# One or two accumulators in memory for the expert blocks of a mixture-of-experts layer

## What is computed

```
def one_block(args):
    tok_b, gate_b, e = args
    xb = xpad[tok_b]
    hb = jax.nn.silu(xb @ w_gate[e]) * (xb @ w_up[e])
    return (hb @ w_down[e]) * gate_b[:, None]

out = lax.map(one_block, ...)
routed = jax.ops.segment_sum(out.reshape(P, D), tok, num_segments=T + 1)[:T]
...
x = x + g2[:, None, :] * (routed + shared).reshape(B, L, D)
...
y = modulate(rms_norm(x, g_final), shf, scf)
```

## Time and profile before

| | us |
|---|---|
| median of 3 runs | 3123.6 (3121.36 to 3126.76) |
| the profiled execution's own time | 3120.24 |
| its span, first to last instruction | 3118.4 |
| PE busy in the span | 2632.8 (84%) |
| DVE busy | 1776.0 (57%) |
| POOL busy | 1143.8 (37%) |
| mean granted TensorE clock | 0.923 |

### The profile page before, as it was taken

How to read it: one execution, slowest core, us unless ns; L and a number is a source line. 1 busy time by engine, 2 the same in 40 slices (tenths; PEclk the granted TensorE clock), 3 DMA queues, 4 the chain that set the end, 5 groups by cost and what they waited for, 6 DMA issues and landing times.

```text
span 3118.4 us, 56271 instructions
## 1 busy us (share of the span) xinstructions
PE 2632.8 (84%) x11753; PEld 2007.4 (64%) x11754; DVE 1776.0 (57%) x3601; ACT 1058.5 (34%) x2213; POOL 1143.8 (37%) x1175
## 2 busy tenths in 40 slices
PE   6896787787686864999999999999999999999930
PEld 1174654554564733887788877778787777878820
DVE  1035776776775855237555466666645644455458
ACT  1021122221121122236444355555544543444411
POOL 0025517547546134333333323333333233333337
PEclk9998898898898676999999999999999999999965
DMA  7861011011010213559787689999987777668665
GB/s 264 316 235 41 14 55 41 23 45 41 21 41 26 96 40 111 142 112 295 219 236 202 189 253 271 266 269 269 269 239 220 222 226 195 189 179 231 155 203 196
DMA packets 255945, 519.10 MB, mean 166 GB/s; under 512 B 18238, under 2 KB 154391, under 8 KB 255732
## 3 DMA queue, kind: packets, MB, share of 16 engines
q1 hardware_dynamic: 199108, 327.34, 30.6%
q0 software_dynamic: 56768, 191.00, 25.4%
HBM read 387.00 MB, written 131.99 MB: 166 GB/s over the span
## 4 chain that ended last, share of the span: by engine, by line
PE 64%; POOL 14%; issue 7%; DVE 5%; DMA 4%; ACT 3%; DVEq 1%; ACTq 1%; SPq 0%; POOLq 0%
PE zb L1479 29%; PE mx L1479 14%; PE zb L1313 7%; POOL b_av L504 7%; PE tp L1492 4%; POOL list_d L514 4%; PE mx L1335 3%; PE zb L1277 2%; DMA b_big<-in_w_ada 2%; DMA b_win<-in_w_down 1%; PE zb L1428 1%; ACT b_wh L802 1%; PE ly L1523 1%; POOL b_pa L487 1%; DVE b_wl L1179 1%
## 5 line engine op out<-in xcount | busy, mean ns | idle before, releaser
L600 POOL DMA_INDIRECT acc_d<-b_ob,b_sidx x180 | 300.2, 1668 | 989.9 <-DVE b_ob L1204 413.7
L1479 PE MATMUL zb<-b_wh,b_xh 128*128 x1448 | 583.0, 403 | 38.7 <-DVE b_wl L1179 17.6
L1479 PE MATMUL zb<-b_wh,b_xl 128*128 x1448 | 567.9, 392 | 0.0
L1179 DVE TENSOR_TENSOR b_wl<-b_win,b_wh (+1 forms) x780 | 481.2, 686 | 152.0 <-ACT b_wh L802 151.8
L1479 PE MATMUL zb<-b_wl,b_xh 128*128 x1448 | 567.0, 392 | 0.0
L802 ACT CAST b_wh<-b_win (+1 forms) x780 | 419.8, 621 | 148.5 <-issue 71.2
L1313 PE MATMUL zb<-b_hT,b_win 128*128 128x256 f32 x1536 | 364.7, 402 | 94.9 <-ACT b_sgt L679 94.1
L1313 PEld LDWEIGHTS zb<-b_hT,b_win 128*128 128x128 f32 x1536 | 310.2, 203 | 148.5 <-ACT b_sgt L679 96.9
L914 DVE SCALAR_TENSOR_TENSOR b_y<-b_a_buf,b_wdw,b_y 128x256 f32<-128x256 f32 x960 | 380.7, 475 | 0.0
L1479 PEld LDWEIGHTS zb<-b_wh,b_xh 128*128 128x128 f32 x1448 | 273.4, 189 | 104.9 <-issue 52.8
L1156 DVE SCALAR_TENSOR_TENSOR b_hh<-b_sgx,b_lt,zb 128x256 f32<-128x256 f32 x181 | 86.7, 479 | 423.4 <-ACT b_sgx L787 422.8
(11 more groups left out here) (242 smaller groups left out, 3295.2 us busy)
## 6 DMA issues: line engine op xcount, KB each, us to landing
b_win<-in_w_gate SPq DMA_DIRECT2D x64, 1024.0 KB
b_win<-in_w_up SPq DMA_DIRECT2D x64, 1024.0 KB
b_win<-in_w_down SPq DMA_DIRECT2D x64, 1024.0 KB
b_big<-in_w_ada SPq DMA_DIRECT2D x12, 2048.0 KB, 9.0
acc_d<-b_x1b SPq DMA_DIRECT2D x1, 9216.0 KB, 35.3
b_xin<-in_x_prompt SPq DMA_DIRECT2D x16, 512.0 KB, 3.2
b_big<-in_w_ada_final SPq DMA_DIRECT2D x4, 2048.0 KB, 8.1
b_xres<-in_x_prompt SPq DMA_DIRECT2D x16, 512.0 KB
```

The costliest lines, as they stand in the source:

```text
L600: G.indirect_dma_start(acc_d, bass.IndirectOffsetOnAxis(ap=sidx[i][:, 0:1], axis=0), ob[i][:], None, compute_op=ALU.add).then_inc(S["scatb ...
L1179: V.tensor_tensor(wl[:, at, :], stage[:, at, :], wh[:, at, :].bitcast(F32), ALU.subtract).then_inc(S["w_lo"], 1)
L1479: last = M.matmul(o, lhs, rhs, start=(first and n == 0), stop=(final and n == len(terms) - 1))
```

## The change

There are now two tensors in memory, `acc_d[0]` and `acc_d[1]`. A block with an even number adds to the first, one with an odd number to the second, each with its own semaphore `scatb[h]`. POOL's wait ahead of an add is for the last add into the same tensor, which is two blocks back. The waits of the copies to `ob` are for the same add as before, counted on the semaphore of its own tensor. Both tensors are zeroed in the front, one DMA after the other, and the final stage loads a tile of each (`fa`, `fb`) and adds the two on DVE ahead of `gated`. No instruction changes its place among the others on any engine; what is added is one zeroing DMA, one load per tile, and one DVE addition per tile.

```
-    acc_d = dram("acc_d", (TROWS, D))
+    acc_d = [dram("acc0_d", (TROWS, D)), dram("acc1_d", (TROWS, D))]
...
-        sp.dma_start(acc_d.rearrange("(t p) n -> p t n", p=P),
-                     x1b[:, :].unsqueeze(1).to_broadcast([P, TROWS // P, D])).then_inc(S["zero_st"], 16)
+        for t in acc_d:
+            sp.dma_start(t.rearrange("(t p) n -> p t n", p=P),
+                         x1b[:, :].unsqueeze(1).to_broadcast([P, TROWS // P, D])).then_inc(S["zero_st"], 16)
...
-        sp.wait_ge(S["scatb"], turns * 32)
+        for t in S["scatb"]:
+            sp.wait_ge(t, turns * 16)
...
-            sp.dma_start(fa[j][0:nt, :], acc_d[ds(i * P, nt), :]).then_inc(S["fin_in"][j], 16)
+            sp.dma_start(fa[j][0:nt, :], acc_d[0][ds(i * P, nt), :]).then_inc(S["fin_in"][j], 16)
+            sp.dma_start(fb[j][0:nt, :], acc_d[1][ds(i * P, nt), :]).then_inc(S["fin_in"][j], 16)
             sp.dma_start(fx[j][0:nt, :], x1_d[ds(i * P, nt), :]).then_inc(S["fin_in"][j], 16)
...
-        added = Goal(pool, "pool_added", 64, 16)
+        added = [Goal(pool, f"pool_added{i}", 32, 16) for i in range(2)]
...
                 if isinstance(q, int):
-                    wait(pool, S["scatb"], 16 * (b - 1))
+                    wait(pool, S["scatb"][h], 16 * ((b - 1) // 2))
                 else:
-                    added.wait(S["scatb"])
-                G.indirect_dma_start(acc_d, bass.IndirectOffsetOnAxis(ap=sidx[i][:, 0:1], axis=0),
-                                     ob[i][:], None, compute_op=ALU.add).then_inc(S["scatb"], 16)
+                    added[h].wait(S["scatb"][h])
+                G.indirect_dma_start(acc_d[h], bass.IndirectOffsetOnAxis(ap=sidx[i][:, 0:1], axis=0),
+                                     ob[i][:], None, compute_op=ALU.add).then_inc(S["scatb"][h], 16)
...
-                wait(act, S["scatb"], 16 * (b - NX))
+                wait(act, S["scatb"][h], 16 * (2 * q + half + 1 - NX // 2))
...
-            dve.wait_ge(S["fin_in"][j], 32 * loads)
+            dve.wait_ge(S["fin_in"][j], 48 * loads)
+            chain(V.tensor_tensor(fa[j][0:nt, :], fa[j][0:nt, :], fb[j][0:nt, :], ALU.add))
             V.tensor_tensor(fa[j][0:nt, :], fa[j][0:nt, :], g2_[:], ALU.mult).then_inc(S["f_gated"], 1)
```

More of the change, by code:

```diff
@@ L150, in program @@
         pool_const dve_const sm_x sm_h sm_state sm_y edge_tp edge_ready
-        cnt_filled cnt_ready row_in table_in tables_ready w_landed w_hi w_lo scatb gu_filled sg_ready hh_ready
+        cnt_filled cnt_ready row_in table_in tables_ready w_landed w_hi w_lo gu_filled sg_ready hh_ready
         gx_filled gx_hi gx_lo ht_filled ht_hi ht_lo o_filled o_act o_dve f_gated f_sum f_sq f_ms f_rs f_aff f_y""".split()
     S = {n: sem(n) for n in names}
-    for n in ("ada_in", "adab_in", "xin_in", "scat"):
+    for n in ("ada_in", "adab_in", "xin_in", "scat", "scatb"):
         S[n] = [sem(f"{n}0"), sem(f"{n}1")]
@@ L230, in program @@
     fin = ExitStack()
-    fa, fx, fy = ([sb(f"{n}{i}", [P, D], F32, fin) for i in range(FB)] for n in ("fa", "fx", "fy"))
+    fa, fb, fx, fy = ([sb(f"{n}{i}", [P, D], F32, fin) for i in range(FB)] for n in ("fa", "fb", "fx", "fy"))
     gfb = sb("gfb", [P, D], F32, fin)
@@ L389, in _ @@
         front_stored(sp)
-        sp.wait_ge(S["zero_st"], 32)
+        sp.wait_ge(S["zero_st"], 48)
         sp.wait_ge(S["scat"][0], 16 * TOPK * (NSUP + 1))
@@ L1036, in step @@
                     bcast(h2)
-                    dve.wait_ge(S["zero_st"], 32)
+                    dve.wait_ge(S["zero_st"], 48)
                 for j in range(TPS):
@@ L1202, in turn @@
                 dve.wait_ge(S["o_filled"], b)
-                wait(dve, S["scatb"], 16 * (b - NX))
+                wait(dve, S["scatb"][h], 16 * (2 * q + half + 1 - NX // 2))
                 V.tensor_copy(ob[i][:, 512:1024], mx[1][:]).then_inc(S["o_dve"], 1)
```

## The result

The change makes the kernel slower: the median went from 3122.48 us (4 runs) to **3155.86 us** (4 runs, 3150.48 to 3158.58). The ratio is 1.0105, with an interval of 1.0085 to 1.0125. The forecast was 3169.2 in a range of 3150 to 3181, so sign and range held, and the number was 13 us too high. The profiled execution took 3154.84 us (span 3153.0, granted clock 0.916), against 3120.24 before, so it can stand for the runs.

The account below looks back on a forecast made before the run. The prediction took PE to bound the expert part, token-tile loads the front and DVE the final stage. The profiled 3120.2 us + 0 + 22.9 + 22.7 = 3165.8, plus 3.4 to the median, gave 3169.2, range 3150 to 3181.

Parts of the forecast that it names:

- The second zeroing, +22.9: Front: another 9.437 MB at 413 GB/s queue ahead of the token tiles, and all engines take over the 22.9 us shift.
- The final stage, +22.7: Final stage, paced by DVE: start 3.8 us later, then 15 periods each 1.26 us longer, 7.40 us a tile.
- a second collision: Final stage rival: POOL and DVE collide twice a tile, the addition takes 3.25 us instead of 1.22; 3200 us, chance 0.02.
- a stage bound by its loads: Final stage rival: the DMAs, at 256 GB/s, set a tile's pace at 8.2 us; 3181 us, chance 0.06.
- The expert part, expected 0: Expert part: removing POOL's wait for the add one block back gains nothing, as PE paces this part.
- the allowance of -15 to +10: Expert part: room around the expected 0, for a gain of 15 us or a loss of 10 us.
- Who waits for the adds? The copies to `ob`: Expert part: copies need the add of four blocks earlier; ACT waits so 4 times in 180 blocks, 10.4 us in sum.
- POOL has spare time: Expert part: besides 391.3 us for adds, POOL waits 413.7 us for PE's output, copied by DVE.
- The second rival: Expert part: a part of PE's idle time, 20 us, comes back, giving 3149 us; chance 0.06.
- the 111 us: Final stage, expected profile: time from the first to the sixteenth `scaled`, instead of 92 us.
- The block's 9.8 us stay: Expert part, expected profile: the time per block, and PE's busy share, do not change.
- The sign of being wrong: Expert part: the forecast is wrong if PE's idle time there falls by more than 15 us.

Follow-up runs that it names:

- e1: Kernel before with a second, unused tensor of 9.4 MB zeroed in the same place: 3141.43 us, ratio 1.0060.
- e5: Changed kernel with the second zeroing issued behind the first step's token tile loads instead of ahead of them: 3133.35 us, ratio 1.0037 to the kernel before.
- e2: Kernel before with the changed final stage, loading each tile of the one accumulator twice and adding the two: 3143.06 us, ratio 1.0068.
- e3: Changed kernel with both tensors and its waits, but one zeroing, one load per tile and no addition: 3109.85 us, ratio 0.9960 to the kernel before.
- e4: Changed kernel whose adds also wait for the last add into the other tensor, so they run one by one: 3166.54 us, ratio 1.0137 to the kernel before.
- e11: Kernel before with POOL's next gather and token-number copies moved ahead of its wait for the last add, behind the wait for ob: 3115.97 us, ratio 0.9985.
- e6: Kernel before with half the columns of every expert's weights loaded: 3132.62 us, ratio 1.0033.
- e7: e3 with half the columns of every expert's weights loaded: 3117.03 us, ratio 0.9988 to the kernel before.
- e8: Changed kernel with late second zeroing, and PE summing the two accumulators' tiles in PSUM in place of DVE's addition: 3125.09 us, ratio 1.0013 to the kernel before.

## Why the prediction was right, and where it was not

**The second zeroing, +22.9: right.** Measured +22.6 to the first add after and +22.4 in e1. Taking the rate of the first one with full DMA engines as the second one's price gave the right number, and the reading that nothing behind the token tiles had slack held. e5 shows the cause: the same bytes behind the tiles cost nothing.

**The final stage, +22.7: right.** Measured +23.1, and +22.9 in e2. The pace came out at 7.40 us as forecast, since POOL's turn moved to `gated` instead of coming twice, and the start at +4.2 for +3.8. The share of the DMA engines was 0.81 for an expected 0.84. The rivals of a second collision and of a stage bound by its loads did not come in.

**The expert part, expected 0: the term that was mis-sized.** It measured -11.1 us, inside the allowance of -15 to +10, and e3 and e4 show that it belongs to the wait. Two sentences of the working failed. "Who waits for the adds? The copies to `ob`" looked only at who waits for the add to *land*. Held with the add was also all that POOL has to do next, and that does not appear as a wait for an add anywhere; e11 shows that it is worth about half of the 11 us. And "POOL has spare time" is true, but its time has a place: when its gather is issued late, it falls on DVE's reads of the block table ahead of the rounding. Even of the copies' waits the working took only ACT's 10.4 us; DVE's copy waits for adds too, 9.0 us in 4 places. The second rival, a part of it comes back, was right in kind (POOL gathers later) with 11 us in place of 20; I gave it too little with 0.06. The reason given for 0 doesn't hold; the allowance around it does.

What the expected profile said of POOL's waits, of ACT's square, of the first `scaled` and of the 111 us came in. "The block's 9.8 us stay" did not quite: 1740.8 / 179 is 9.73. The sign of being wrong set for this part, over 15 us less idle time of PE, was all but met, with 14.8. What stays open is how the 11 us reach PE, through late splits or, as e6 and e7 suggest, through late weights; what the other half of them is that e11 did not bring; and why e6 and e7 got slower with half the bytes.

## What to carry to other kernels

A long wait on an engine with spare time can still cost something. Ask not only who waits for the waiting instruction's result, but what else stands behind it in its queue and where that work lands when it is late; moving that work ahead of the wait (e11) gave about half the gain of a second accumulator, by the medians, without its zeroing, loads and additions. Price a doubled resource by its setup and its merge: here each cost 23 us, twice the gain, the setup only for standing ahead of two small loads (e5), the merge for falling on the engine that set the pace.

## What was not expected of the hardware

- A store of 9.4 MB from SBUF to memory held 413 to 417 GB/s with the DMA engines full, and two loads of 0.5 MB that were issued 8.3 us before it landed came 7.2 us behind it: ACT's idle time ahead of the token tiles went from 0.74 to 24.52 us.
- A sequencer's read of one number from SBUF takes DVE 0.31 us, and up to 1.58 us beside an indirect DMA: 55 of the 63 slow ones of the kernel before fell in the 2.1 us from the start of a gather.
- In the final stage's mix of loads and stores the DMA engines moved 311 GB/s in e8, at a share of 0.83, and a load landed as fast as at 277 GB/s and 0.81 (6.6 against 6.5 us).
- With one operand of `gated` in PSUM, POOL's `fy` beside it took 2.34 us in place of 3.25, which is also the shortest of the changed kernel's 16. The timeline of e8:
```profile
3040.73 2.34 POOL L621 TENSOR_TENSOR b_fy<-b_fa,b_Bfb 128x1024 f32<-128x1024 f32 x1 [1.40 <-DVE b_fa L1244]
```
- Two accumulating scatters in flight landed no slower than one at a time (median 6.4 against 6.5 us).
- Half the columns of the weights, half the bytes, made the expert part 13.1 us longer (e6) and 6.8 us longer (e7).
